# The delta rule's scan: query-state products moved behind the product with w, state update released by the key-value products

## The reference

```python
def step(state, inp):
    u_i, w_i, qg_i, kd_i, att_i, dl_i = inp
    v_new = u_i - w_i @ state                 # "bhcd,bhde->bhce"
    o = qg_i @ state + att_i @ v_new
    state = state * dl_i[..., None, None] + kd_i.T @ v_new
    return state, o
```

## Time and profile before

| | |
|---|---|
| median of three executions | 2515.05 us (2512.92 to 2515.93) |
| span of the profiled execution, first to last instruction | 2513.4 us |
| time of the profiled execution itself | not given; only its span |
| TensorE busy | 2479.0 us, 99% of the span, 15346 instructions |
| VectorE busy | 1622.7 us, 65% |
| ScalarE busy | 1209.6 us, 48% |
| GpSimd busy | 75.9 us, 3% |
| mean granted TensorE clock | 0.997 of full speed |
| stretch of the scans | 1668.4 to 1950.8 us |
| TensorE busy in 1660 to 1960 us | 289.00 of 300 us |

### The profile page before, as it was taken

How to read it: one execution, slowest core, us unless ns; L and a number is a source line. 1 busy time by engine, 2 the same in 40 slices (tenths; PEclk the granted TensorE clock), 3 DMA queues, 4 the chain that set the end, 5 groups by cost and what they waited for, 6 DMA issues and landing times.

```text
span 2513.4 us, 37708 instructions
## 1 busy us (share of the span) xinstructions
PE 2479.0 (99%) x15346; PEld 2065.3 (82%) x15346; DVE 1622.7 (65%) x2583; ACT 1209.6 (48%) x2027; POOL 75.9 (3%) x114
## 2 busy tenths in 40 slices
PE   9999999999999999999999999999999999999998
PEld 7999888887878778878999888777776788888887
DVE  6888348866765555348887257766877655677733
ACT  6555334765546465245555246544333454444421
POOL 0111000000000000000110000000000000000000
PEclk9999999999999999999999999999999999999999
DMA  5675332222212222233775322211111112333232
GB/s 166 179 181 156 109 100 85 84 76 76 83 65 72 76 68 80 89 101 93 176 185 149 100 90 96 76 43 35 43 43 51 59 59 84 99 94 101 88 101 72
DMA packets 80525, 237.82 MB, mean 95 GB/s; under 512 B 8928, under 2 KB 10976, under 8 KB 80352
## 3 DMA queue, kind: packets, MB, share of 16 engines
q1 hardware_dynamic: 68832, 213.56, 26.5%
q0 software_dynamic: 10080, 18.35, 4.7%
q10 hardware_dynamic: 1440, 3.49, 0.4%
HBM read 233.27 MB, written 2.10 MB: 94 GB/s over the span
## 4 chain that ended last, share of the span: by engine, by line
PE 93%; DVE 4%; ACT 1%; DMA 1%; issue 1%; SPq 0%; ACTq 0%; DVEq 0%
PE bank L2311 22%; PE bank L2313 21%; PE bank L2312 21%; PE bank L2325 4%; PE bank L2327 4%; PE bank L2326 4%; PE bank L2580 2%; PE bank L2505 1%; PE bank L2411 1%; PE bank L2513 1%; PE bank L2499 1%; PE bank L2676 1%; PE bank L2486 1%; DVE hl L3094 1%; PE bank L2340 0%
## 5 line engine op out<-in xcount | busy, mean ns | idle before, releaser
L2311 PE MATMUL bank<-uR,hl 128*128 128x512 f32 x1684 | 683.4, 406 | 5.1 <-DVE uR L3105 3.2
L3094 DVE TENSOR_TENSOR hl<-raw,hl 128x1024 fp32r<-128x1024 f32 (+2 forms) x325 | 385.8, 1190 | 445.1 <-ACT hl L2725 443.8
L2313 PE MATMUL bank<-uR,hl 128*128 128x512 f32 x1684 | 658.0, 391 | 0.0
L2312 PE MATMUL bank<-uR,hl 128*128 128x512 f32 x1684 | 657.5, 390 | 0.0
L2725 ACT CAST hl<-raw 128x1024 fp32r<-128x1024 f32 (+2 forms) x325 | 329.8, 1020 | 204.8 <-PE bank L2313 196.1
L2311 PEld LDWEIGHTS bank<-uR,hl 128*128 128x128 f32 x1684 | 317.0, 188 | 93.9 <-issue 23.6
L2313 PEld LDWEIGHTS bank<-uR,hl 128*128 128x128 f32 x1684 | 316.7, 188 | 68.3
L2312 PEld LDWEIGHTS bank<-uR,hl 128*128 128x128 f32 x1684 | 317.3, 188 | 66.5 <-issue 6.0
L3088 DVE TENSOR_TENSOR hl<-raw,hl 128x1024 fp32r<-128x1024 f32 (+1 forms) x142 | 150.7, 1075 | 35.6 <-ACT hl L2721 32.4
L2325 PE MATMUL bank<-sum,hl 128*128 128x256 f32 x560 | 158.8, 284 | 2.5 <-DVE fA L3272 2.5
L2326 PE MATMUL bank<-sum,hl 128*128 128x256 f32 x560 | 158.5, 283 | 0.0
(11 more groups left out here) (521 smaller groups left out, 4337.4 us busy)
## 6 DMA issues: line engine op xcount, KB each, us to landing
raw<-in_win SPq DMA_DIRECT2D x147, 512.0 KB, 3.5
raw<-in_w SPq DMA_DIRECT2D x44, 512.0 KB, 3.5
raw<-in_w1u SPq DMA_DIRECT2D x54, 256.0 KB, 3.0
raw<-in_w2u SPq DMA_DIRECT2D x51, 256.0 KB, 3.1
raw<-in_w1g SPq DMA_DIRECT2D x22, 512.0 KB, 4.8
raw<-in_w2g SPq DMA_DIRECT2D x22, 512.0 KB, 4.5
raw<-in_w1d SPq DMA_DIRECT2D x16, 512.0 KB, 3.5
raw<-in_wssd SPq DMA_DIRECT2D x16, 512.0 KB, 3.6
```

What stands on the lines that cost most here:

```text
L2311: e.matmul(s.bank[:, :], h[:, 0, w], hi, start=s.first and q == 0, stop=False)
L2312: e.matmul(s.bank[:, :], h[:, 0, w], lo, start=False, stop=False)
L2313: i = e.matmul(s.bank[:, :], h[:, 1, w], hi, start=False, stop=s.last and q == n - 1)
L3094: e.tensor_tensor(h[:, 1, w], x[:, w], h[:, 0, w].bitcast(F), ALU.subtract).then_inc(*sig("dve_split.lo", s, i))
```

## The change

The matmuls of `q` x state move from the end of `scan_s` to `scan_v`, right behind `w` x state, with a signal of their own (`pe_gdn.qS`). The output bank is taken before `scan_v`, which so asks for two side banks (one at chunk 0), and `scan_s` asks for two. The state updates wait for `pe_gdn.kv` and `pe_gdn.qS`, no longer for `pe_gdn.o`. The prices of both steps in the planner's table change.

```diff
--- before.py
+++ after.py
@@ -236,8 +236,8 @@
     "gdn_fold": [("PE", 2.14, "pe_gdn.fold"), ("DVE", 0.69, "dve_gdn.T"), ("DVE", 0.69, "dve_gdn.U")],
     "gdn_u": [("PE", 1.95), ("ACT", 0.6, "act_gdn.u", 0), ("ACT", 0.6, "act_gdn.u", 1)],
     "gdn_w": [("PE", 1.93), ("ACT", 0.6, "act_gdn.w", 0), ("ACT", 0.6, "act_gdn.w", 1)],
-    "scan_v": [("PE", 0.4), ("DVE", 0.3, "dve_gdn.vn")],
-    "scan_s": [("PE", 1.1, "pe_gdn.o"), ("DVE", 0.35, "dve_gdn.state", 0), ("DVE", 0.35, "dve_gdn.state", 1),
+    "scan_v": [("PE", 0.7), ("DVE", 0.3, "dve_gdn.vn")],
+    "scan_s": [("PE", 0.75, "pe_gdn.o"), ("DVE", 0.35, "dve_gdn.state", 0), ("DVE", 0.35, "dve_gdn.state", 1),
                ("DVE", 0.6, "dve_gdn.o")],
     "gdn_norm": [("ACT", 1.25), ("DVE", 1.0, "dve_gdn.sum"), ("ACT Ln", 0.45), ("DVE", 1.4, "dve_gdn.on")],
     "gdn_out": [("PE", 1.6), ("DVE", 1.9, "dve_gdn.out")],
@@ -1972,15 +1972,16 @@
         before = None
         for c in range(C8):
             if c:
-                yield from ready(("dve_gdn.state", before, 1), ("dve_gdn.state", before, 0), *w, banks=1)
-            b = SB.take() if c else None
-            s = step("scan_v", c=c, w=w, u=u, b=b, st=st_, vn=vn, before=before)
+                yield from ready(("dve_gdn.state", before, 1), ("dve_gdn.state", before, 0), *w, banks=2)
+            else:
+                yield from ready(*w, banks=1)
+            b, bo = SB.take() if c else None, SB.take()
+            s = step("scan_v", c=c, w=w, u=u, q=q, b=b, bo=bo, st=st_, vn=vn, before=before)
             if c:
                 b.release(("dve_gdn.vn", s))
-            yield from ready(("dve_gdn.vn", s), *u, *kd, banks=3)
+            yield from ready(("dve_gdn.vn", s), *u, *kd, banks=2)
             bs = [SB.take() for _ in range(2)] if c < C8 - 1 else []
-            bo = SB.take()
-            s2 = step("scan_s", c=c, p=p, q=q, kd=kd, att=att, bs=bs, bo=bo, st=st_, vn=vn, u=u, o=o, s=s, before=before,
+            s2 = step("scan_s", c=c, p=p, kd=kd, att=att, bs=bs, bo=bo, st=st_, vn=vn, u=u, o=o, s=s, before=before,
                       cols=S2["cols"])
             for i, x in enumerate(bs):
                 x.release(("dve_gdn.state", s2, i))
@@ -2629,6 +2630,10 @@
                 after(*s.w[i].t)
                 t = e.matmul(s.b[HALF[i], 0:128], s.w[i][:, s.c * 64:s.c * 64 + 64], s.st[:, tcol(i)], start=True, stop=True)
             t.then_inc(*sig("pe_gdn.wS", s))
+            after(*s.q[0].t, *s.q[1].t, *s.bo.after)
+            for i in range(2):
+                t = e.matmul(s.bo[HALF[i], 0:128], s.q[i][:, s.c * 64:s.c * 64 + 64], s.st[:, tcol(i)], start=True, stop=True)
+            t.then_inc(*sig("pe_gdn.qS", s))
 
         def scan_s(s):
             c, at, to = s.c, slice(s.c * 64, s.c * 64 + 64), tcol(s.c % 4)
@@ -2642,10 +2647,7 @@
                 for i, r in enumerate(HALF):
                     t = e.matmul(s.bs[i][:, 0:128], s.kd[c // 4][r, to], v[r, :], start=True, stop=True)
                 t.then_inc(*sig("pe_gdn.kv", s))
-            after(*s.bo.after, *s.att.t, *s.q[0].t, *s.q[1].t)
-            if c:
-                for i in range(2):
-                    e.matmul(s.bo[HALF[i], 0:128], s.q[i][:, at], s.st[:, tcol(i)], start=True, stop=True)
+            after(*s.bo.after, *s.att.t)
             for r in HALF:
                 t = e.matmul(s.bo[r, 128:256], s.att[r, at], v[r, :], start=True, stop=True)
             t.then_inc(*sig("pe_gdn.o", s))
@@ -3623,7 +3625,8 @@
             c, to = s.c, tcol(s.c % 4)
             if c < C8 - 1:
                 go.wait_ge(*on("pe_gdn.kv", s))
-                go.wait_ge(*on("pe_gdn.o", s))
+                if c:
+                    go.wait_ge(*on("pe_gdn.qS", s.s))
                 go.wait_ge(*on("act_gdn.dl", s.cols))
                 if c == 0:
                     after(*s.st.after)
```

## The result

The changed kernel is slower: 2522.97 us (2520.65 to 2525.51, 4 runs) against 2514.5 us for the kernel before on the same chip, a ratio of 1.0037 with a 95% interval of 1.0023 to 1.0052. That is 8.5 us more, where 3.0 us less was forecast. The profiled execution took 2520.65 us with a span of 2518.8 us, 1.85 us around it.

A forecast was written before the change was run, and what follows sets the result against it. The prediction took TensorE, busy 99%, to bound the kernel, with few holes. From 2515.05 us it took 2.2 us for TensorE's neighbours, 0.8 for VectorE's updates and 0 for order: 2512.0 us, range 2504 to 2521 leaving out 2 in 10.

The forecast's parts named there:

- Term 1: TensorE in the scan: query-state product beside w x state saves 0.11 us a chunk, 2.2 us over 20 chunks.
- the best case I gave: TensorE's moved product costs only 0.24 us as in L2612's row, saving 0.13 for each of 28 chunks, 3.6 us.
- Rival 1: TensorE's neighbours save nothing: the pair costs 0.74 us, only 0.8 us is left, 2514.2 us; chance 0.14.
- 20 chunks outside the holes: Of 28 chunks, those in stretches where TensorE is full or nearly so, where 0.11 us each counts.
- Term 2: VectorE's state updates in the scan may start up to 0.73 us earlier; bounds 0 to 3.3 us, 0.8 us taken.
- the 0.8 us: Gain from earlier VectorE updates, 1941 to 1951 us: waits of 0.51 and 0.29 us go.
- the 0.29 at 1946.60: Issue time on VectorE in the last scan's chain, claimed to go because key-value is done at 1945.72.
- The 0.51: VectorE's wait before the updates at 1941.94, claimed to go because key-value ended before 1941.43.
- The sum of both: TensorE's 2.2 us and VectorE's 0.8 us together, -3.0 us, giving 2512.0 us.
- the third: The planner's written order: chunks and projections may change places; effect taken as 0 as a mean.
- Rival 2: TensorE's holds get shorter as the scan ends sooner and the clock stays up: 2507.7 us; chance 0.26.
- Rival 3: A hold gets longer because the bank taken at w x state is missing: 8.5 us lost, 2520.6 us; chance 0.18.

The follow-up runs named there:

- programs_only: Changed engine programs with all steps in the order of the kernel before, planner decisions replayed; 2510.73 us, ratio 0.9988 to the kernel before.
- banks_only: Kernel before with only the changed requests for side banks, prices and engine programs as before; 2522.63 us, ratio 1.0036 to the kernel before.
- prices_only: Kernel before with only the two changed lines of the planner's price table; 2527.57 us, ratio 1.0057 to the kernel before.
- covered_rounds: Changed engine programs, planned with old prices and bank requests, each search round placed only behind a main-stream step; 2527.74 us, ratio 1.0056 to the kernel before.
- hold_rounds: Changed kernel, planner places no search round of block 3 while the last pair's scan runs; 2521.39 us, ratio 1.0034 to the kernel before.
- rounds_behind: Changed programs in the old order, three search rounds between the last scan's last two chunks moved behind the last; 2509.94 us, ratio 0.9986 to the kernel before.

## Why the prediction was wrong, point by point

- **What bounds the kernel** was right: TensorE, and the loss is holes and clock between 1660 and 2030 us.
- **Term 1, the neighbours on TensorE**, was right, and larger: 0.15 us a chunk instead of 0.11, above the best case I gave (0.13, from L2612, whose groups are of another form, 64x64), since the second group of a form costs 0.22 and not 0.26. The rule that weight loads don't overlap with matmuls of the same rows (the Trainium skill, TensorE: Matmul & The Clock Gate, "Packing small matmuls") is not what this trace shows: L2635's weight load starts at 1747.96 with L2631's matmul, both of all 128 rows, and its group costs 0.22 us behind L2631's. Rival 1 falls. At 20 chunks outside the holes, 0.15 gives 3.0 us.
- **Term 2, the updates on VectorE**: they start earlier, as stated (idle time 6.3 to 1.8 us in the old order), but the 0.8 us did not come. In programs_only TensorE still waits 1.9 us for updates, where it was 1.4, and 1.6 for the last subtraction, where it was 1.9. Of the 0.8, the 0.29 at 1946.60 was misread: VectorE was not waiting then but busy with L3763, the first row below, from before. The 0.51 shrank to 0.17 in programs_only (before the update at 1936.92), but nothing came of it: in the second row, from programs_only, VectorE idles 0.62 us for ScalarE, does the same instruction, and only then the next update (at 1942.45), 1.0 us after its kv ended. The last scan's chunk is made by VectorE's other work.

```profile
1946.28 0.69 DVE L3763 SCALAR_TENSOR_TENSOR fB<-fB 128x512 f32<-128x512 f32 x1
```

```profile
1941.85 0.69 DVE L3780 SCALAR_TENSOR_TENSOR fB<-fB 128x512 f32<-128x512 f32 x1 [0.62 <-ACT fB L2718]
```

- **The sum of both**, -3.0, is what programs_only measured (-2.85, interval -5.3 to -0.8 us by its ratio), by 3.0 + 0 rather than 2.2 + 0.8. That the two misses cancel is luck, and the split is worked out, not measured apart.
- **The step that failed** is the third: "I take 0 for the order as a mean". The changed order measured +12.4 us under the old programs and 11.3 under the new, and every other order that the planner made 9 to 18, each against the old order with the same programs. That is what turned -2.85 into +8.5. The mean was not 0 because the order before was not one draw of many alike: of eight planned orders it is the fastest, by 9 us or more with the same programs. How it came to be so good no run shows. The prediction also summed the prices wrongly (in the first chunk they fall by 0.05 us too, +0.30 and -0.35), but the forecast used no number from this.
- **Rival 2** fell: no hold got shorter. **Rival 3** has the side and nearly the size (2520.6; measured 2522.97), and in part the place: the end of the last scan grew, while the hold that it was priced from, the third scan's, hardly did (6.1 us of holes from 1860 to 1900, before 5.3). Its mechanism, a missing side bank, is not shown as the cause. On the chip no moved product waits for its bank, and of the preparation's levels only L2581 waits for the scan's update and copy, 2.5 us of 22.9. In the planner the requests for banks are one way to a worse order (banks_only, 9.4 us) and the prices another (prices_only, 14.7 us, banks as before). With a chance of 0.18 for it and a range up to 2521 I gave the order far too little.

What stays open is which choices in an order cost the time in the early scans (3.6 us more holes from 1660 to 1740 us in the changed kernel). In the written order of the changed kernel 13 steps of the first scan, with 13 rounds, stand in a row without a projection, in the kernel before 10 with 9; covered_rounds speaks for the rounds, but no run takes length and rounds apart. The runs show that it is order, not which choice in it.

## What to carry to other kernels

Where a planner fixes the order of work, a change of its prices, buffers or waits is a change of its own: hold the old order, by replaying its decisions, and measure the new instructions in it. Here all seven other planned orders were worse, so 0 is no safe guess for a new order. A queue that serves both the slow side chain and the operands of the bound engine (VectorE here) has two sides: in each of three tries work moved out of the scans' way (hold_rounds, covered_rounds, rounds_behind) brought a new wait behind it.

## What the runs showed of the hardware that I had not expected

- A small matmul group behind one of the same form (128 rows x 64 columns of weights, 128 columns streamed, two halves side by side) costs 0.22 us, and 0.37 behind another form, at full clock. Its weights load while matmuls of the same rows run (1747.96).
- Holes are paid twice: from 1945 to 1960 us the granted clock was 0.59, 0.50 and 0.54, and a projection behind another took 0.43 us (1956.62) where it takes 0.23.
- One wait of 19.3 us arose from the place of VectorE instructions of at most 1.3 us in its queue (covered_rounds).
